# Gated linear recurrence of a two-block model: the diagonal step's products are issued ten weight chunks later, beside the third and fourth level

## The chip, the cores and the metric

The kernel runs on one core of one Trainium2 chip. The metric is the device time of one execution in microseconds (us). It is the median of three executions: 1901.26 us, from 1900.43 to 1902.49.

## The reference

The whole program is two transformer-like blocks over 256 tokens of width 2048: a convolution mixer, a recurrent mixer (HGRN2), windowed attention and a gated feed-forward layer. All matrix products are float32. The change is in the recurrent mixer alone, which is, for each of 16 heads of width 128, run once forwards and once backwards over the tokens:

```
def step(state, inp):
    qb, kb, vb, fb = inp
    b = jnp.cumsum(fb, axis=2)
    o_inter = jnp.einsum("bhtk,bhkv->bhtv", qb * jnp.exp(b), state)
    diff = b[:, :, :, None, :] - b[:, :, None, :, :]
    decay = jnp.exp(jnp.where(lower_tri, diff, -jnp.inf))
    scores = jnp.einsum("bhtk,bhsk,bhtsk->bhts", qb, kb, decay)
    o_intra = jnp.einsum("bhts,bhsv->bhtv", scores, vb)
```

The score of a pair of tokens is a product of query and key with a decay between them for every one of the 128 channels. Its diagonal (a token with itself) has no decay.

## The kernel before, in words

**The stream of weights.** Nearly the whole time goes into products of activations (256 tokens) with large weight matrices. A weight matrix is read in chunks of 256 rows by 512 columns; every chunk is one 512 KB transfer into one of four buffers `raw`. ScalarE rounds a chunk to `w_hi` (line 877), VectorE forms the rest `w_lo` (line 1261), and TensorE issues twelve matmuls for it (lines 619 to 621) into `acc`: two row tiles by two token tiles by three products (hi with hi, low with hi, hi with low). So TensorE may start a chunk when `split_ready` says that its `w_lo` is there, and ScalarE may round one when TensorE has left the chunk four before it.

**Hooks.** All else is hung between the chunks by hand. Each engine has its own table: `put(8, f)` runs `f` after the engine has issued its part of chunk 8 of a group of 32 chunks; numbers from 32 on fall in the next group. ScalarE and VectorE run some two to four chunks ahead of TensorE, so the same step has different numbers on different engines.

**The recurrence.** The 16 heads go in four groups `j` of four heads. The projections of group `j` are the 32 chunks of phase `hgrn` (use `j`); its recurrence is worked in the 32 chunks behind those (`process(j)`), thus beside the projections of group `j + 1`, and for the last group beside phase `hgrn_z`. VectorE first turns the raw projections (`quarters`, hooks 28, 30, 31, line 1549), GpSimd moves their blocks (`moves`, line 502), ScalarE makes gates and logarithms out of them (`gates`, `ln_f`, `ln_k`, lines 1046 to 1063), VectorE makes running sums (line 1442, 1449) and keys (1457, 1459). The pairs of tokens are then covered by eight levels and the diagonal. Level 1 is the pairs across the two halves of the sequence, level 2 those of neighbouring blocks of 64 tokens, level 3 of 32, down to level 8 of single tokens. For a level VectorE makes exponents (`diffs`), ScalarE takes their exponential (`exp`), VectorE weighs them with the queries (`weigh`, line 1499), TensorE forms the products (`level`, line 736; level 1 line 727), and the result is taken out of PSUM by ScalarE (`take`, lines 1089 to 1100, levels 0 to 3) or by VectorE under a mask (line 1508, levels 4 to 8). "Level 0" is the diagonal: its operand is made by `diagonal` on VectorE at hook 6, its products are 32 matmuls of 32x32 on TensorE at hook 8, and `take(j, 0)` on ScalarE at hook 11 copies them to `SB`, on which the masked copies of the levels from 4 on are laid. On TensorE level 1 stands at hook 13, level 2 at 14, levels 3 and 4 at 18, levels 5 and 6 at 22, levels 7 and 8 at 26 together with `av_across`, and `av` at 28.

Order between engines is held by semaphores that count: `g_G` operands weighed, `g_mm` levels multiplied, `g_S` levels taken, `g_M` moves of GpSimd. Operand buffers are `E` and `E_more` with two places each, chosen by `operands(s)`; before the change level 0 shares the second place of `E` with level 2. The PSUM tensor `T` has four banks: level 1 fills banks 0 and 1, the levels from 2 on alternate between banks 2 and 3, and level 0 uses bank 2.

Of the kernel before, what the change touches and what calls it, by code (L numbers as in the profile page):

```python
# [30 lines left out]
ACT = mybir.ActivationFunctionType  # L31
ALU = mybir.AluOpType
# [4 lines left out]
S = 256  # L37
# [127 lines left out]
def build(nc, t, out):  # L165
    ph = phases()
    ctx = ExitStack()
    with ctx:
# [75 lines left out]
        ssh = sb(hs, "ssh", [P, 3, 2 * HPG])  # L244
        powers = sb(hs, "powers", [P, 2 * HPG])
        gate_rows = (aftok, abtok, qtok, sz)
        lf_back = qtok[:, :, :].rearrange("p a (b c) -> p (a b) c", c=S)
        hs.close()

# [29 lines left out]

        def operands(s):  # L280

            b = (s - 1) % 4 if s else 1
            return (E_more if b >= 2 else E)[:, b % 2, :, :, :]

        def gate_banks(k):
            return T01 if k % 2 else T23
# [282 lines left out]
        def _(pe):  # L569
# [145 lines left out]
            def level(j, s):  # L715

                pe.wait_ge(g_G, 9 * j + s + 1)
                if s == 0:
                    pe.wait_ge(g_M, 3 * j + 3)
                if s >= 2:  # L720
                    pe.wait_ge(g_K, 7 * j + s - 1)
                    pe.wait_ge(g_S, 9 * j + s - 1)
                e = operands(s)
                for h in range(HPG):
                    for b in range(2):
                        if s == 1:
                            last = nc.tensor.matmul(T[:, h // 2, (h % 2) * S + b * P:(h % 2) * S + b * P + P],  # L727
                                                    e[:, 0, h, b * P:(b + 1) * P], e[:, 1, h, (1 - b) * P:(2 - b) * P],
                                                    start=True, stop=True)
                            continue  # L730
                        n = HB if s == 2 else QUARTER
                        for i in range(P // n):
                            at = b * P + i * n
                            to = b * P + (i ^ 1) * n if s in (2, 3) else at
                            g, q = (e[:, 1, h, at:at + n], qT[:, h, to:to + n]) if s == 0 else (e[:, 0, h, at:at + n], e[:, 1, h, to:to + n])
                            last = nc.tensor.matmul(T[i * n:(i + 1) * n, 2 + s % 2, (2 * h + b) * n:(2 * h + b + 1) * n],  # L736
                                                    g, q, start=True, stop=True)
                last.then_inc(g_mm, 1)

# [10 lines left out]

            def av_across(j):
                pe.wait_ge(g_raw, 4 * j + 4)
                pe.wait_ge(g_S, 9 * j + 2)
                av_products(True)

            def av(j):
# [2 lines left out]

            def process(j):  # L760

                at = Hooks().put(8, lambda: level(j, 0))
                for s in range(1, 9):
                    at.put(13 if s == 1 else 10 + 4 * (s // 2 + s % 2) if s > 2 else 14, lambda s=s: level(j, s))
                return at.put(26, lambda: av_across(j)).put(28, lambda: av(j))
# [98 lines left out]
        def _(act):  # L864
# [219 lines left out]

            def take(j, s):

                act.wait_ge(g_mm, 9 * j + s + 1)
                if s == 0:
                    A(SB[:, :, :, :].rearrange("p a b c -> p (a b c)"), T[:, 2, 0:S], ACT.Copy).then_inc(g_S, 1)
                    return  # L1090
                if s == 1:
                    if not is_first(j):
# [24 lines left out]
            def process(j):  # L1117
                at = Hooks().put(1, lambda: gates(j, 0)).put(6, lambda: gates(j, 1))
                for d in range(2):
                    at.put(6 + d, lambda d=d: ln_f(j, d)).put(8 + d, lambda d=d: ln_k(j, d))  # L1120
                at.put(11, lambda: take(j, 0)).put(12, lambda: cross_keys(j)).put(13, lambda: cross_queries(j))
                for s in range(1, 9):
                    if s > 1:
                        at.put(14 if s == 2 else 11 + 2 * s, lambda s=s: exp(j, s))
                    if s < ACT_TAKES:
                        at.put((15, 17, 20)[s - 1], lambda s=s: take(j, s))
                return at.put(29, lambda: blocks(j)).put(31, lambda: o_out(j))
# [112 lines left out]
        def _(dve):  # L1240
# [185 lines left out]
            def diagonal(j):  # L1426

                dve.wait_ge(g_lb, j + 1)
                dve.wait_ge(g_act, 6 * j + 2)
                for h in range(HPG):  # L1430
                    V.tensor_scalar(E[:, 1, 1, h, :], kf[:, h, :], lbj[:, 0, 1, h:h + 1], None, ALU.mult)
                settle()
                for h in range(HPG):
                    last = STT(out=E[:, 1, 1, h, :], in0=kb[:, h, :], scalar=lbj[:, 1, 1, h:h + 1],
                               in1=E[:, 1, 1, h, :], op0=ALU.mult, op1=ALU.add)
                last.then_inc(g_G, 1)

            def scan_f(j):
# [39 lines left out]
            def diffs(j, s):  # L1478

                e = operands(s)  # L1480
                dve.wait_ge(g_mm, 9 * j + max(1, s - 3))
                c = width(s)
                rf, rb = bounds(c)
                fr, bl = halves(Bc[:, :, :], c)[1], halves(Xc[:, :, :], c)[0]
# [16 lines left out]
            def take(j, s):  # L1501

                settle()
                if s == ACT_TAKES:
                    dve.wait_ge(g_S, 9 * j + s)
                dve.wait_ge(g_mm, 9 * j + s + 1)
                V.memset(none[:, :], 0.0)
                V.copy_predicated(SB[:, :, :, :].rearrange("p a b c -> p (a b) c"),
                                  lmask[:, s - ACT_TAKES, :].unsqueeze(1).to_broadcast([P, 8, QUARTER]),
# [301 lines left out]
```

## Time and profile before

| | |
|---|---|
| median of three executions | 1901.26 us |
| the profiled execution's own time | 1900.38 us |
| its span, first to last instruction | 1898.1 us |
| TensorE busy | 1892.3 us |
| VectorE, ScalarE, GpSimd busy | 1286.2, 1057.5, 613.3 us |

TensorE is recorded as busy over nearly the whole span. A matmul of the weight stream is recorded for 0.39 us, while the next one starts 0.23 us after it: records overlap, so a short wait of TensorE does not always show as idle time, and is better read from the distance of starts. Weight loads into the array (PEld) are recorded apart; idle time before one of them names what it waited for. A small float32 matmul of the levels is recorded twice, so a level of 32 shows as 64 records.

### The profile page before, as it was taken

The page shows a single profiled execution, that of the slowest core. Times are in us where ns is not written, and L with a number is a line of the kernel's source. Part 1 is how long each engine was busy: PE and PEld are TensorE (multiplying, and loading weights), DVE is VectorE, ACT ScalarE, POOL GpSimd, SP SyncE. Part 2 cuts the span into 40 slices and gives each one's busy share as a digit, 9 for nine tenths or more (in the row PEclk, how much of TensorE's full clock was granted, in tenths as well). Part 3 has the DMA queues.
Part 4 walks back from the last instruction along what each step waited for, and adds up shares of the span by engine and source line. Part 5 has one row for each costly group of instructions (what it writes and reads, how often), then busy time and mean ns, then how long its engine had stood idle before and what let it go on. Part 6 is the DMA issues. An engine that isn't in the chain of part 4 may idle for free.

```text
span 1898.1 us, 28814 instructions
## 1 busy us (share of the span) xinstructions
PE 1892.3 (100%) x10864; PEld 1560.7 (82%) x10864; DVE 1286.2 (68%) x1869; ACT 1057.5 (56%) x1401; POOL 613.3 (32%) x641
## 2 busy tenths in 40 slices
PE   9999999999999999999999999999999999999999
PEld 8888878888887888888887888888888888888887
DVE  5899967545888888887668876555555555544443
ACT  7444466455868787875465755444444444443432
POOL 1899852406051423302418641122222222210000
PEclk9999999999999999999999999999999999999999
DMA  9666556666555565555565455666666666666564
GB/s 324 192 190 188 178 167 195 193 189 188 167 166 170 155 186 162 175 160 185 189 190 151 151 177 169 208 190 197 189 190 197 192 195 190 195 192 196 191 195 159
DMA packets 183166, 352.62 MB, mean 186 GB/s; under 512 B 11792, under 2 KB 12304, under 8 KB 183056
## 3 DMA queue, kind: packets, MB, share of 16 engines
q1 hardware_dynamic: 182912, 351.12, 60.7%
q8 instruction: 72, 1.18, 0.3%
q14 instruction: 38, 0.31, 0.1%
q10 hardware_dynamic: 144, 0.01, 0.0%
HBM read 348.99 MB, written 2.10 MB: 185 GB/s over the span
## 4 chain that ended last, share of the span: by engine, by line
PE 91%; DVE 3%; POOL 2%; ACT 1%; issue 1%; DMA 1%; DVEq 1%; POOLq 0%; ACTq 0%; SPq 0%
PE acc L619 29%; PE acc L621 29%; PE acc L620 29%; PE T L736 1%; PE T L575 1%; DVE w_lo L1261 1%; POOL apad L524 1%; POOL kb L502 1%; DMA raw<-in_conv_w_in_dram 1%; DVEq L1247 1%; ACT w_hi L877 0%; POOL kf L502 0%; PE T L837 0%; PE T L727 0%; PE T L746 0%
## 5 line engine op out<-in xcount | busy, mean ns | idle before, releaser
L1261 DVE TENSOR_TENSOR w_lo<-raw,w_hi 128x1024 fp32r<-128x1024 f32 x564 | 695.3, 1235 | 518.6 <-ACT w_hi L877 510.7
L877 ACT ACTIVATE w_hi<-raw 128x1024 fp32r<-128x1024 f32 x656 | 688.9, 1058 | 610.8 <-PE acc L621 585.6
L619 PE MATMUL acc<-w_hi,h_hi 128*128 128x512 f32 x1872 | 736.0, 393 | 0.9 <-DVE w_lo L1261 0.8
L621 PE MATMUL acc<-w_hi,h_lo 128*128 128x512 f32 x1872 | 729.4, 390 | 0.0
L620 PE MATMUL acc<-w_lo,h_hi 128*128 128x512 f32 x1872 | 729.2, 390 | 0.0
L619 PEld LDWEIGHTS acc<-w_hi,h_hi 128*128 128x128 f32 x1872 | 351.6, 188 | 80.0 <-issue 5.8
L621 PEld LDWEIGHTS acc<-w_hi,h_lo 128*128 128x128 f32 x1872 | 351.5, 188 | 73.6
L620 PEld LDWEIGHTS acc<-w_lo,h_hi 128*128 128x128 f32 x1872 | 351.7, 188 | 71.1
L564 POOL COPY fT<-fq 32x256 f32<-32x256 f32 x176 | 110.8, 630 | 398.9 <-DVE fq L1743 392.0
L473 POOL TENSOR_TENSOR w_lo<-raw,w_hi 128x1024 fp32r<-128x1024 f32 x80 | 190.3, 2405 | 71.2 <-ACT w_hi L877 71.2
L1352 DVE SCALAR_TENSOR_TENSOR T<-vpad,feat,T 128x256 f32<-128x256 f32 x464 | 182.5, 485 | 0.0
L619 PE MATMUL acc<-w_hi,y_hi 128*128 128x512 f32 x384 | 151.1, 394 | 0.1
L620 PE MATMUL acc<-w_lo,y_hi 128*128 128x512 f32 x384 | 149.6, 390 | 0.0
L620 PE MATMUL acc<-w_lo,f_hi 128*128 128x512 f32 x352 | 137.0, 389 | 0.0
L619 PE MATMUL acc<-w_hi,f_hi 128*128 128x512 f32 x352 | 137.0, 389 | 0.0
L621 PE MATMUL acc<-w_hi,f_lo 128*128 128x512 f32 x352 | 137.0, 389 | 0.0
L502 POOL COPY kf<-sz 32x256 f32<-32x256 f32 x64 | 37.2, 582 | 279.1 <-DVEq L1247 276.6
L621 PE MATMUL acc<-w_hi,hy_lo 128*128 128x512 f32 x256 | 99.8, 390 | 0.0
L619 PEld LDWEIGHTS acc<-w_hi,y_hi 128*128 128x128 f32 x384 | 72.1, 188 | 17.0 <-issue 1.2
L620 PEld LDWEIGHTS acc<-w_lo,y_hi 128*128 128x128 f32 x384 | 72.2, 188 | 14.5
L621 PEld LDWEIGHTS acc<-w_hi,f_lo 128*128 128x128 f32 x352 | 66.1, 188 | 13.8
L619 PEld LDWEIGHTS acc<-w_hi,f_hi 128*128 128x128 f32 x352 | 66.1, 188 | 13.7
(252 smaller groups left out, 1553.8 us busy)
## 6 DMA issues: line engine op xcount, KB each, us to landing
raw<-in_hgrn_w_in_dram SPq DMA_DIRECT2D x160, 512.0 KB, 3.7
raw<-in_conv_w_in_dram SPq DMA_DIRECT2D x96, 512.0 KB, 4.2
raw<-in_ffn_w_gate_dram SPq DMA_DIRECT2D x88, 512.0 KB, 4.3
raw<-in_ffn_w_up_dram SPq DMA_DIRECT2D x88, 512.0 KB, 4.2
raw<-in_ffn_w_down_dram SPq DMA_DIRECT2D x88, 512.0 KB, 4.6
raw<-in_attn_w_qkv_dram SPq DMA_DIRECT2D x40, 512.0 KB, 3.8
raw<-in_conv_w_out_dram SPq DMA_DIRECT2D x32, 512.0 KB, 4.5
raw<-in_hgrn_w_out_dram SPq DMA_DIRECT2D x32, 512.0 KB, 3.9
```

Of the source, the lines that this page charges most:

```text
L473: nc.gpsimd.tensor_tensor(w_lo[:, slot, :, :], raw[:, slot, :, :], rounded(w_hi[:, slot, :, :]), ALU.subtract).then_inc(split_ready, 1)
L502: last = nc.gpsimd.tensor_copy(turned_block(dst, a, b), own_block(src, a, b))
L524: nc.gpsimd.tensor_copy(vrows[a * QUARTER:(a + 1) * QUARTER, b::4, :], kvtok[b * QUARTER:(b + 1) * QUARTER, :, KVH * HD:])
L564: last = nc.gpsimd.tensor_copy(turned_block(fT, a, b), own_block(fq, a, b))
L575: last = nc.tensor.transpose(dst[:, q // 2, at:at + P], src[:, tb, q * P:(q + 1) * P], ident[:, :])
L619: nc.tensor.matmul(o, hi[:, kt, a], w_hi[:, slot, kk, :], start=c == 0 and kk == 0, stop=False)
L620: nc.tensor.matmul(o, hi[:, kt, a], w_lo[:, slot, kk, :], start=False, stop=False)
L621: last = nc.tensor.matmul(o, lo[:, kt, a], w_hi[:, slot, kk, :], start=False, stop=c == p.chunks - 1 and kk == CK - 1)
L736: last = nc.tensor.matmul(T[i * n:(i + 1) * n, 2 + s % 2, (2 * h + b) * n:(2 * h + b + 1) * n], g, q, start=True, stop=True)
L877: A(w_hi[:, slot, :, :], raw[:, slot, :, :], ACT.Copy).then_inc(hi_ready, 1)
L1261: TT(w_lo[:, slot, :, :], raw[:, slot, :, :], rounded(w_hi[:, slot, :, :]), ALU.subtract).then_inc(split_ready, 1)
L1352: STT(out=cy[:, kt, :] if tap == TAPS - 1 else y, in0=v, scalar=w, in1=y, op0=ALU.mult, op1=ALU.add).then_inc(c_tap, 1)
```

## The change

The diagonal's products move on TensorE from hook 8 to hook 18, where they stand ahead of levels 3 and 4, and its copy on ScalarE from hook 11 to hook 20, ahead of the copy of level 3. The operand gets a buffer of its own (`same`, laid over the scratch tensor `fg`, not used otherwise in this stretch) and the products go to bank 0 of `T`, which is free once level 1 has been taken. Since `g_mm` and `g_S` count in order of issue, a function `place(s)` now gives the rank of a level: 1, 2, 0, 3, 4 and so on. VectorE's `diffs(j, 2)` no longer waits for level 0.

```
 def operands(s):
-    b = (s - 1) % 4 if s else 1
+    b = (s - 1) % 4
+def place(s):
+    return {1: 1, 2: 2, 0: 3}.get(s, s + 1)
...
 # TensorE, level(j, s)
                 if s == 0:
                     pe.wait_ge(g_M, 3 * j + 3)
+                    pe.wait_ge(g_S, 9 * j + place(1))
                 if s >= 2:
                     pe.wait_ge(g_K, 7 * j + s - 1)
-                    pe.wait_ge(g_S, 9 * j + s - 1)
+                    if s > 4:
+                        pe.wait_ge(g_S, 9 * j + place(s - 2))
+                    elif s > 2:
+                        pe.wait_ge(g_S, 9 * j + place(2))
+                    elif j:
+                        pe.wait_ge(g_S, 9 * j)
...
-                            g, q = (e[:, 1, h, at:at + n], qT[:, h, to:to + n]) if s == 0 else ...
-                            last = nc.tensor.matmul(T[i * n:(i + 1) * n, 2 + s % 2, ...
+                            g, q = (same[:, h, at:at + n], qT[:, h, to:to + n]) if s == 0 else ...
+                            last = nc.tensor.matmul(T[i * n:(i + 1) * n, 2 + s % 2 if s else 0, ...
...
 # TensorE, process(j)
-                at = Hooks().put(8, lambda: level(j, 0))
+                at = Hooks().put(18, lambda: level(j, 0))
...
 # ScalarE, take(j, s) and process(j)
-                act.wait_ge(g_mm, 9 * j + s + 1)
+                act.wait_ge(g_mm, 9 * j + place(s))
...
-                at.put(11, lambda: take(j, 0))
+                at.put(20, lambda: take(j, 0))
...
 # VectorE, diagonal(j): E[:, 1, 1, h, :] becomes same[:, h, :]; diffs(j, s):
-                dve.wait_ge(g_mm, 9 * j + max(1, s - 3))
+                if s > 4:
+                    dve.wait_ge(g_mm, 9 * j + place(s - 4))
```

On TensorE, before, at the first of the four groups: the diagonal's 32 matmuls (operands `qT` and `E`) stand alone behind chunk 8 of the weight stream.

```order
L620 MATMUL acc<-w_lo,h_hi 128x512
L621 MATMUL acc<-w_hi,h_lo 128x512
L736 MATMUL T<-qT,E 32x32 x32
L619 MATMUL acc<-w_hi,h_hi 128x512
L620 MATMUL acc<-w_lo,h_hi 128x512
```

On TensorE, after, behind chunk 18 of the same group: the diagonal's 32 matmuls (now with operand `fg`) are followed at once by the 32 of level 3 and the 32 of level 4, which the order shows as one row of 64 (`E_more`).

```order
L626 MATMUL acc<-w_hi,h_lo 128x512
L747 MATMUL T<-qT,fg 32x32 x32
L747 MATMUL T<-E_more 32x32 x64
L624 MATMUL acc<-w_hi,h_hi 128x512
L625 MATMUL acc<-w_lo,h_hi 128x512
```

So of two interruptions of the weight stream one is gone, and the other holds 96 small matmuls in place of 64.

On ScalarE, before, the copy into `SB` stands between the rounding of chunks 11 and 12, and the four pieces of level 3 (into `ST`) stand alone between the rounding of chunks 20 and 21.

```order
L877 ACTIVATE w_hi<-raw 128x1024
L1089 ACTIVATE SB<-T 128x256
L877 ACTIVATE w_hi<-raw 128x1024
...
L877 ACTIVATE w_hi<-raw 128x1024
L1100 ACTIVATE ST<-T 32x8x32 x4
L877 ACTIVATE w_hi<-raw 128x1024
```

On ScalarE, after, at the second place:

```order
L1094 ACTIVATE E_more<-E_more 128x1024 x2
L888 ACTIVATE w_hi<-raw 128x1024
L1100 ACTIVATE SB<-T 128x256
L1111 ACTIVATE ST<-T 32x8x32 x4
L888 ACTIVATE w_hi<-raw 128x1024
```

The copy now stands ahead of level 3's, and both ahead of the rounding of chunk 21. VectorE and GpSimd issue the same work in the same order as before.

## Rows read from the trace of the kernel before

**Rows 1.** The page: span, TensorE's busy time, the chain that ended last.

```profile
span 1898.1 us, 28814 instructions
...
PE 91%; DVE 3%; POOL 2%; ACT 1%; issue 1%; DMA 1%; DVEq 1%; POOLq 0%; ACTq 0%; SPq 0%
```

**Rows 2.** Timeline, TensorE, level 0 of the first group: start us, length us, instruction.

```profile
477.68 0.39 PE L620 MATMUL acc<-w_lo,h_hi 128*128 128x512 f32 x1
...
482.66 0.39 PE L621 MATMUL acc<-w_hi,h_lo 128*128 128x512 f32 x1
482.98 0.76 PE L736 MATMUL T<-qT,E 128*32 128x32 f32 x64
483.68 0.50 PE L619 MATMUL acc<-w_hi,h_hi 128*128 128x512 f32 x1
...
484.25 0.40 PE L621 MATMUL acc<-w_hi,h_lo 128*128 128x512 f32 x1
```

**Rows 3.** Timeline, TensorE, levels 3 and 4 of the first group.

```profile
513.91 0.39 PE L621 MATMUL acc<-w_hi,h_lo 128*128 128x512 f32 x1
514.23 1.37 PE L736 MATMUL T<-E_more 128*32 128x32 f32 x128
...
516.09 0.39 PE L621 MATMUL acc<-w_hi,h_lo 128*128 128x512 f32 x1
```

**Rows 4.** Waits before weight loads, 684 to 700 us: us in total, times, longest.

```profile
PEld acc L619 <- DVE w_lo L1261: 0.7, 2, 0.4
```

**Rows 5.** Timeline, TensorE, second group: start of chunks 10 and 13.

```profile
585.92 0.39 PE L621 MATMUL acc<-w_hi,h_lo 128*128 128x512 f32 x1
586.75 0.50 PE L619 MATMUL acc<-w_hi,h_hi 128*128 128x512 f32 x1 [0.44 <-DVE w_lo L1261]
...
594.84 0.39 PE L621 MATMUL acc<-w_hi,h_lo 128*128 128x512 f32 x1
595.28 0.50 PE L619 MATMUL acc<-w_hi,h_hi 128*128 128x512 f32 x1
```

**Rows 6.** Timeline, TensorE, first group: start of chunk 13.

```profile
494.71 0.39 PE L619 MATMUL acc<-w_hi,h_hi 128*128 128x512 f32 x1
```

**Rows 7.** Timeline, VectorE, first group: low part of chunk 13, then level 1's weighing.

```profile
492.71 1.22 DVE L1261 TENSOR_TENSOR w_lo<-raw,w_hi 128x1024 fp32r<-128x1024 f32 x1
494.89 1.23 DVE L1499 TENSOR_TENSOR E<-E,qT 128x1024 f32<-128x1024 f32 x1 [0.95 <-ACT E L1076]
```

**Rows 8.** Timeline, VectorE, second group: low parts of chunks 10 and 13.

```profile
585.47 1.23 DVE L1261 TENSOR_TENSOR w_lo<-raw,w_hi 128x1024 fp32r<-128x1024 f32 x1 [0.15 <-issue]
...
594.01 1.22 DVE L1261 TENSOR_TENSOR w_lo<-raw,w_hi 128x1024 fp32r<-128x1024 f32 x1
```

**Rows 9.** Timeline, ScalarE and VectorE, behind level 3 of the first group.

```profile
515.03 1.54 ACT L1100 ACTIVATE ST<-T 32x256 f32<-32x256 f32 x4 [1.90 <-PE T L736]
...
517.69 1.23 DVE L1261 TENSOR_TENSOR w_lo<-raw,w_hi 128x1024 fp32r<-128x1024 f32 x1 [0.79 <-ACT w_hi L877]
```

**Rows 10.** Stretches: us, then PE, PEld, DVE, ACT, POOL busy (count), PEclk, DMA share, GB/s.

```profile
517.60:541.60 24.00, 24.00 (x356) 19.92 (x355) 23.45 (x32) 17.30 (x19) 0.00 (x0) 1.00 0.56 157
541.60:569.00 27.40, 27.40 (x135) 23.08 (x133) 20.29 (x23) 17.18 (x21) 25.70 (x34) 1.00 0.55 164
569.00:595.30 26.30, 25.81 (x172) 20.09 (x170) 21.56 (x32) 24.74 (x44) 7.67 (x16) 1.00 0.54 169
```

**Rows 11.** Timeline, ahead of the second group's gates: VectorE's turning, GpSimd, ScalarE.

```profile
540.28 1.30 DVE L1549 STREAM_TRANSPOSE sz<-aftok 128x512 f32<-128x512 f32 x2
...
541.67 9.63 POOL L502 COPY kf<-sz 32x256 f32<-32x256 f32 x16 [67.49 <-DVEq L1247]
...
568.97 1.06 ACT L1046 ACTIVATE qtok<-kb 128x1024 f32<-128x1024 f32 x1 [1.64 <-POOL kb L502]
```

**Rows 12.** Timeline, ScalarE, first group: the diagonal's copy, and the next wait.

```profile
485.23 0.36 ACT L1089 ACTIVATE SB<-T 128x256 f32<-128x256 f32 x1
...
489.11 0.40 ACT L1070 ACTIVATE E<-kf,Bc 128x128 f32<-128x128 f32 x1 [1.27 <-DVEq L1247]
```

More of the change, by code:

```diff
@@ L246, in build @@
         gate_rows = (aftok, abtok, qtok, sz)
+        same = fg[:, :, :].rearrange("p a (b c) -> p (a b) c", c=S)
         lf_back = qtok[:, :, :].rearrange("p a (b c) -> p (a b) c", c=S)
@@ L734, in level @@
                             to = b * P + (i ^ 1) * n if s in (2, 3) else at
-                            g, q = (e[:, 1, h, at:at + n], qT[:, h, to:to + n]) if s == 0 else (e[:, 0, h, at:at + n], e[:, 1, h, to:to + n])
-                            last = nc.tensor.matmul(T[i * n:(i + 1) * n, 2 + s % 2, (2 * h + b) * n:(2 * h + b + 1) * n],
+                            g, q = (same[:, h, at:at + n], qT[:, h, to:to + n]) if s == 0 else (e[:, 0, h, at:at + n], e[:, 1, h, to:to + n])
+                            last = nc.tensor.matmul(T[i * n:(i + 1) * n, 2 + s % 2 if s else 0, (2 * h + b) * n:(2 * h + b + 1) * n],
                                                     g, q, start=True, stop=True)
@@ L752, in av_across @@
                 pe.wait_ge(g_raw, 4 * j + 4)
-                pe.wait_ge(g_S, 9 * j + 2)
+                pe.wait_ge(g_S, 9 * j + place(0))
                 av_products(True)
@@ L1085, in take @@
             def take(j, s):
-                act.wait_ge(g_mm, 9 * j + s + 1)
+                act.wait_ge(g_mm, 9 * j + place(s))
                 if s == 0:
-                    A(SB[:, :, :, :].rearrange("p a b c -> p (a b c)"), T[:, 2, 0:S], ACT.Copy).then_inc(g_S, 1)
+                    A(SB[:, :, :, :].rearrange("p a b c -> p (a b c)"), T[:, 0, 0:S], ACT.Copy).then_inc(g_S, 1)
                     return
@@ L1120, in process @@
                     at.put(6 + d, lambda d=d: ln_f(j, d)).put(8 + d, lambda d=d: ln_k(j, d))
-                at.put(11, lambda: take(j, 0)).put(12, lambda: cross_keys(j)).put(13, lambda: cross_queries(j))
+                at.put(20, lambda: take(j, 0)).put(12, lambda: cross_keys(j)).put(13, lambda: cross_queries(j))
                 for s in range(1, 9):
@@ L1430, in diagonal @@
                 for h in range(HPG):
-                    V.tensor_scalar(E[:, 1, 1, h, :], kf[:, h, :], lbj[:, 0, 1, h:h + 1], None, ALU.mult)
+                    V.tensor_scalar(same[:, h, :], kf[:, h, :], lbj[:, 0, 1, h:h + 1], None, ALU.mult)
                 settle()
                 for h in range(HPG):
-                    last = STT(out=E[:, 1, 1, h, :], in0=kb[:, h, :], scalar=lbj[:, 1, 1, h:h + 1],
-                               in1=E[:, 1, 1, h, :], op0=ALU.mult, op1=ALU.add)
+                    last = STT(out=same[:, h, :], in0=kb[:, h, :], scalar=lbj[:, 1, 1, h:h + 1],
+                               in1=same[:, h, :], op0=ALU.mult, op1=ALU.add)
                 last.then_inc(g_G, 1)
@@ L1504, in take @@
                 if s == ACT_TAKES:
-                    dve.wait_ge(g_S, 9 * j + s)
-                dve.wait_ge(g_mm, 9 * j + s + 1)
+                    dve.wait_ge(g_S, 9 * j + place(s - 1))
+                dve.wait_ge(g_mm, 9 * j + place(s))
                 V.memset(none[:, :], 0.0)
```

## The prediction

> **What bounds the kernel now.** I read the page first. The span is 1898.1 us and the chain that ended last is 91% TensorE [rows 1]: whatever is put into TensorE's row of work, or taken out, is time, unless TensorE waits somewhere near. So the second question is where TensorE waits around the moved step. Busy shares don't tell it, since records overlap; I went through the starts of its matmuls in the timeline.
>
> The undisturbed pace: 22 matmuls from 477.68 to 482.66 [rows 2], 0.226 us each, thus 2.72 us for a chunk of twelve.
>
> Where it waits: in the first of the four groups chunk 13 starts in step. In the second, chunk 10 starts 0.83 us behind the matmul before it and chunk 13 0.44 us [rows 5]; without the pace that is 0.60 and 0.21 us, plus 0.11 us each time because a first matmul behind a pause is recorded with 0.50 us where others have 0.39. The third group has two such waits for `w_lo`, 0.7 us together before the weight loads [rows 4], and the same view of 784 to 800 us gives the same row for the fourth. These are waits for VectorE, which finishes `w_lo` of chunk 13 at 594.01 + 1.22 = 595.23 us [rows 8]; TensorE starts 0.05 us later.
>
> What makes VectorE late there is what the forecast hangs on. I followed it backwards.
> - At 515.03 ScalarE takes level 3 of the first group, having waited 1.90 us for TensorE, and VectorE's next low part waits 0.79 us for ScalarE [rows 9].
> - From there VectorE is busy 23.45 of 24.00 us [rows 10], up to the turning at 540.28 [rows 11]; GpSimd, which had waited 67.49 us for that, starts at once and is busy 25.70 of 27.40 us [rows 10]; ScalarE waits 1.64 us for it until 568.97 [rows 11], and is itself busy 24.74 of 26.30 us up to chunk 13 of the second group [rows 10].
>
> So from level 3 of one group (TensorE's hook 18) to chunk 13 of the next, some 80 us, there is a second chain beside TensorE without room in it, and in groups two to four it is the longer one. From chunk 13 to hook 18 TensorE itself is the longer. The two form a circle.
>
> **The change part by part.**
>
> *Removed at hook 8.* From the last matmul before level 0 to the third behind it are 484.25 - 482.66 = 1.59 us [rows 2]; less three of the pace (0.68) the interruption costs 0.91 us. In group one TensorE then reaches chunk 13 0.91 us earlier than 494.71 [rows 6]. But `w_lo` of that chunk is done at 492.71 + 1.22 = 493.93 [rows 7], and with the 0.05 us above the start can be at 493.98 at the earliest. That gives 0.73 us, less 0.11 for starting behind a pause: 0.62 us gained. Does VectorE come earlier too? It doesn't wait for level 0 here, and ScalarE, which loses a copy of 0.36 us, next stands 1.27 us waiting for VectorE [rows 12]. So no. In groups two to four TensorE already waits for the same chunk, so 0.91 us less of work is 0.91 us more of waiting, mostly at chunk 10: gained 0.
>
> Level 1 behind chunk 13: it needs the weighing that ends at 494.89 + 1.23 = 496.12 [rows 7]; TensorE gets there at 493.98 + 0.11 + 12 x 0.226 = 496.80, so nothing new is late. The cover is 0.68 us thick.
>
> *Added at hook 18.* Levels 3 and 4 in one interruption cost 516.09 - 513.91 = 2.18 less 0.68, thus 1.50 us [rows 3]. One level alone costs 0.91, so a further one in the same interruption costs 0.59 us, and 0.32 us is the price of interrupting. The recorded lengths say the same: 0.76 us for 64 records, 1.37 us for 128 [rows 2, 3]. A third level of the same shape I take at 0.59, the nearest row; it would cost 0 if it hid wholly beside the others, for which no row speaks, and 0.91 us if it paid as one alone.
>
> Here the rule of the Trainium skill (TensorEngine Tiling (Array Packing), Key Properties) says that a change of tiling mode drains the TensorE. The trace agrees with it in kind: a level that joins others pays 0.32 us less than one alone. By that rule by itself, with TensorE as the only bound, the sum would be four times 0.32 us less; it is the first rival below.
>
> *Where the added 0.59 us goes.* Level 3 ends 0.59 us later relative to chunk 13, since level 0 now stands in front of it, and level 3's end is where the second chain begins. So all of that chain moves: chunk 13 of the next group comes 0.59 us later than it would.
>
> *The copy on ScalarE.* It now stands between the wait and level 3's copies, in the chain. It takes 0.36 us [rows 12] and can begin as soon as level 0 is done, 0.59 us before level 3 is; it is over 0.2 us before ScalarE is wanted. I cost it at nothing; uncovered it would be 0.36 us a group.
>
> *Waits.* Level 0's new wait is for the copy of level 1, five chunks back. Level 3 waits for the copy of level 2, as level 4 did directly behind it. On VectorE a wait that was never felt is gone. All nothing. Operand and bank are of the same kind and size as before.
>
> *Sum.* Group one: -0.62 + 0.59 = -0.03 us. Groups two, three and four: +0.59 us each, because nothing is gained at hook 8 and the circle or, behind the last, TensorE itself carries the addition to the end. Together +1.74 us. Against the profiled execution (1900.38 us, of which 1898.1 is span) that is 1902.1 us; the median of the runs is 0.88 us above that execution, so I put 1901.26 + 1.74 = 1903.0 us.
>
> **The rivals.**
>
> *The interruption is saved everywhere.* If the second chain has room that I don't see, TensorE alone counts: four times 0.32 us, thus -1.3 us, 1900.0 us. For it: group one does have 0.73 us of room. Against it: the waits of TensorE for `w_lo` in groups two to four. Chance 0.12.
>
> *Some of both.* The shift at hook 18 is swallowed in one or two groups by small gaps of the second chain (0.55 us of VectorE's 24.00 are not busy, mostly drains), so that the sum ends near 0: 1901.3 us. Chance 0.08.
>
> *The copy is not covered.* If ScalarE comes to level 3 late by the whole copy, 4 x 0.36 us more: +3.2 us, 1904.4 us. It decides where level 0's end and level 3's end lie less than 0.36 us apart. The pace of the small matmuls speaks against it. Chance 0.07.
>
> *Slower by more than the measurement's grain.* In group two TensorE would stand still at chunk 10 for 0.44 + 0.91 = 1.35 us instead of the 0.44 of [rows 5]. If its clock fell there from 2.4 to 1.2 GHz, each us of matmuls would take two. With +1.7 us already there, a further 2.1 us is needed for 0.2%, so 2.1 us of work at the low level; at 4 us of it the time is about 1905 us, and more if the shorter pauses of the third and fourth group do it too. Against it: the granted clock is 1.00 in the stretch with the pauses of today [rows 10]. Chance 0.03.
>
> *Forecast:* the second chain passes the addition on, +1.7 us. Chance 0.70, own range 1902.0 to 1904.2.
>
> **How the numbers follow.** A change of under 0.2% (3.8 us) can't be told from none by a measurement of this kernel. The forecast and the first three rivals lie inside it: 0.97, of which I give 0.03 to what I haven't thought of. Slower by over 0.2%: the clock, and the far end of the uncovered copy, 0.05. Faster: 0.01. No change: 0.94. The range runs from a little below the first rival, since medians of three move by about 1 us, to a little over the uncovered copy: 1899.6 to 1905.0.
>
> **What the changed profile would show.** TensorE waits at chunk 10 of groups two to four for 0.9 us longer than before, and in group one for the first time at chunk 13, some 0.2 us. The interruption at hook 18 costs 2.1 us net of the pace. ScalarE's `SB` copy ends before level 3's matmuls do. The distance from level 3 of one group to chunk 13 of the next is the same as before to 0.1 us, while that from chunk 13 to level 3 is 0.6 us longer. The forecast is wrong if chunk 13 of the second group comes earlier relative to level 3 of the first, if the three levels cost 0.91 us more than two, or if TensorE's clock is under 1.00 anywhere between 480 and 860 us.

## The result, and the profile after

The changed kernel takes 1908.68 us (median of 6 runs, 1906.29 to 1910.24) beside 1900.50 us of the kernel before (6 runs, 1899.72 to 1902.49): ratio 1.0037, 95% interval 1.0027 to 1.0047. That is slower by more than 0.2%, and outside the range of the prediction (up to 1905.0). The profiled execution took 1909.72 us.

The page of the changed kernel: the span, and the chain that ended last by engine.

```profile
span 1907.1 us, 28812 instructions
...
PE 83%; DVE 5%; POOL 4%; ACT 2%; issue 2%; DVEq 1%; POOLq 1%; DMA 1%; ACTq 0%; SPq 0%
```

The span is 9.0 us longer than that of [rows 1], and TensorE's share of the chain fell from 91 to 83%: more of the way to the end leads through VectorE and GpSimd.

To find the 9.0 us I compared the starts of the first matmul of the same chunk in both timelines:

```
start of                     after minus before, us     added since the row above
group one, chunk 0                 +0.28                (start-up)
group two, chunk 13                +0.34                +0.06
group two, chunk 19                +0.92                +0.58   hook 18
group two, chunk 27                +1.15                +0.23   hook 26
group three, chunk 10              +2.39                +1.24   second chain
group three, chunk 19              +3.03                +0.64   hook 18
group four, chunk 10               +4.12                +1.09   second chain
group four, chunk 19               +4.73                +0.61   hook 18
group four, chunk 23               +9.04                +4.31   behind hook 18
end of the span                    +8.97
```

Three rows at hook 18 are the predicted ones. Nearly half of the loss stands in one place behind hook 18 of the fourth group, and 2.3 us in the second chain, whose length the prediction had taken as fixed.

**The place in the fourth group.** Timeline of TensorE, changed kernel; the number in brackets is the idle time ahead of a row and what ended it.

```profile
820.98 0.39 PE L626 MATMUL acc<-w_hi,h_lo 128*128 128x512 f32 x1
821.21 0.40 PE L624 MATMUL acc<-w_hi,h_hi 128*128 128x512 f32 x1
824.01 0.50 PE L625 MATMUL acc<-w_lo,h_hi 128*128 128x512 f32 x1 [2.40 <-issue]
824.35 0.40 PE L626 MATMUL acc<-w_hi,h_lo 128*128 128x512 f32 x1
```

From 821.21 to 824.01 are 2.80 us, less one step of the pace 2.57 us. The releaser is "issue": no semaphore, buffer or bank that the profile shows was awaited. The next view says what did come in that time. DMA queues in the stretch 818 to 826 us, changed kernel: packets, MB, share.

```profile
q8 instruction: 1, 0.02, 0.7%
```

Queue 8 moves nothing but packets of 16,384 bytes. From the first of them to the one at 1264.6 us there are 64, and TensorE has 16,056 recorded instructions (matmuls, weight loads and its sequencer's) in that time: 255 for each packet. So I read a packet as a block of 256 instructions of TensorE's program code. This one started at 821.81 us and took 0.92 us by the DMA's record; TensorE went on 1.3 us after it. The block before had started at 808.63 us.

And behind the stop (the same kernel; stretches with the columns of [rows 10]):

```profile
818.00:821.00 3.00, 3.00 (x198) 2.52 (x197) 3.00 (x5) 1.44 (x4) 0.00 (x0) 1.00 0.77 227
821.00:824.00 3.00, 0.61 (x3) 0.17 (x1) 1.43 (x4) 2.96 (x5) 0.00 (x0) 1.00 0.28 107
824.00:825.00 1.00, 0.99 (x4) 0.85 (x5) 1.00 (x3) 1.00 (x2) 0.00 (x0) 0.95 0.27 33
825.00:827.00 2.00, 2.00 (x6) 1.53 (x6) 2.00 (x3) 0.37 (x1) 0.00 (x0) 0.50 0.82 254
827.00:828.00 1.00, 1.00 (x4) 0.82 (x3) 1.00 (x3) 0.82 (x1) 0.00 (x0) 0.50 0.45 55
...
829.00:832.00 3.00, 3.00 (x15) 2.49 (x14) 2.71 (x4) 2.24 (x3) 0.00 (x0) 1.00 0.47 115
```

After the stop the granted clock goes to 0.50, that is from 2.4 to 1.2 GHz: from 825.17 to 828.15 us the matmuls start 0.43 us apart instead of 0.23. With the slower steps at both ends of it that costs 1.6 us. Stop 2.57, clock 1.6, and 0.11 for starting behind a pause: 4.3 us, the whole row of the table.

**The pieces that the prediction named.** TensorE at hook 18 of the first group, then chunk 13 of the first and chunks 10 and 13 of the second group:

```profile
493.88 0.39 PE L626 MATMUL acc<-w_hi,h_lo 128*128 128x512 f32 x1
494.27 0.50 PE L624 MATMUL acc<-w_hi,h_hi 128*128 128x512 f32 x1
...
513.64 0.39 PE L626 MATMUL acc<-w_hi,h_lo 128*128 128x512 f32 x1
513.96 0.76 PE L747 MATMUL T<-qT,fg 128*32 128x32 f32 x64
514.57 1.35 PE L747 MATMUL T<-E_more 128*32 128x32 f32 x128
...
516.43 0.39 PE L626 MATMUL acc<-w_hi,h_lo 128*128 128x512 f32 x1
...
585.99 0.39 PE L626 MATMUL acc<-w_hi,h_lo 128*128 128x512 f32 x1
587.09 0.50 PE L624 MATMUL acc<-w_hi,h_hi 128*128 128x512 f32 x1 [0.72 <-DVE w_lo L1272]
...
595.16 0.39 PE L626 MATMUL acc<-w_hi,h_lo 128*128 128x512 f32 x1
595.62 0.50 PE L624 MATMUL acc<-w_hi,h_hi 128*128 128x512 f32 x1
```

ScalarE behind hook 18 of the first group, and what it takes there:

```profile
514.76 0.38 ACT L1100 ACTIVATE SB<-T 128x256 f32<-128x256 f32 x1 [1.90 <-PE T L747]
515.36 1.53 ACT L1111 ACTIVATE ST<-T 32x256 f32<-32x256 f32 x4 [0.22 <-PE T L747]
```

Three levels cost 516.43 - 513.64 = 2.79, less 0.68, thus 2.11 us, where two cost 1.50 in [rows 3]: 0.61 us for the third. The copy `SB` ends at 515.14, and ScalarE then waits another 0.22 us for level 3: it is covered. Chunk 13 of the first group starts 0.39 us behind the matmul ahead of it, a new short wait; VectorE's low part of that chunk ran from 492.99 to 494.21.

**The second chain.** The stretches of [rows 10] on its way from level 3 of group one to group two, moved along with it:

```profile
517.93:541.93 24.00, 24.00 (x356) 19.92 (x355) 23.45 (x32) 17.30 (x19) 0.00 (x0) 1.00 0.53 156
541.93:569.33 27.40, 27.40 (x135) 23.08 (x134) 20.29 (x23) 17.16 (x21) 25.71 (x34) 1.00 0.55 166
```

Between groups one and two it is the same chain, to 0.01 us of busy time. Between two and three it is not. GpSimd, and then VectorE, changed kernel:

```profile
667.80 3.27 POOL L507 COPY kb<-aftok 32x256 f32<-32x256 f32 x3
...
669.57 1.23 DVE L1272 TENSOR_TENSOR w_lo<-raw,w_hi 128x1024 fp32r<-128x1024 f32 x1 [0.74 <-ACT w_hi L888]
```

Three copies (the last three of the eight of this half of `kb`) take 3.27 us here; in e6, shown below, the same three take 2.18. The eighth copy started at 669.58 us, 0.01 us behind VectorE's low part of chunk 7, and took 1.49 us. A copy of this shape has two lengths, 0.4 to 0.5 us and 1.3 to 1.5 us: in the profiles of both kernels all 242 long ones started while a VectorE instruction with two inputs was running, and none of the 634 that started without one was long (84 started beside one and were short). In the kernel before, in the same transition, the copy came first and took 0.40, and the half of `kb` 9.10 instead of 10.20 us. Between groups three and four it is the same again, 9.98 for 9.01 us.

### The profile page after: what moved, and what is told of

Its sections match the earlier page's. It is cut to its first block, busy times and chain, and to the rows that moved or that the text cites. A ratio compares the mean times of both kernels' runs of the same rounds, so it can differ in the third digit from the quotient of the medians.

```text
span 1907.1 us, 28812 instructions
## 1 busy us (share of the span) xinstructions
PE 1895.4 (99%) x10864; PEld 1561.2 (82%) x10864; DVE 1286.6 (67%) x1869; ACT 1057.9 (55%) x1401; POOL 613.4 (32%) x641
## 4 chain that ended last, share of the span: by engine, by line
PE 83%; DVE 5%; POOL 4%; ACT 2%; issue 2%; DVEq 1%; POOLq 1%; DMA 1%; ACTq 0%; SPq 0%
PE acc L624 27%; PE acc L626 27%; PE acc L625 27%; POOL kb L507 2%; DVE w_lo L1272 2%; POOL kf L507 1%; DVEq L1258 1%; PE T L580 1%; POOL apad L529 1%; ACT w_hi L888 1%; PE T L747 1%; DMA raw<-in_conv_w_in_dram 1%; PE T L848 0%; PE T L738 0%; DVE Xc L1460 0%
```

## The experiments

Twelve runs. The kernel before is timed beside each set: 1900.64 us with e1 to e4, 1900.83 with e5 to e8, 1901.19 with e9 to e12. In the expectations, A is the theory that program code is late behind long bursts of small matmuls (its rival: a data wait that the changed order makes); D is that the second chain carries additions at hook 18 and TensorE's waits swallow those at hook 8; E that only TensorE's own work counts.

**Where the code stands: e1, e2, e3.** All kernels have the same work in the recurrence; only the position of its instructions in TensorE's code is moved, by tiny matmuls in front of the whole program, of which nothing is read. The shifts were worked out from the recorded instructions: four for a tiny matmul and four for a warming one.

```diff
-WARM = 14
+WARM = 10
+EXTRA = 36
...
+                for i in range(EXTRA):
+                    nc.tensor.matmul(T[0:QUARTER, 0, 0:QUARTER], ones[:, 0:QUARTER], ones[:, 0:QUARTER], start=True, stop=True)
```

e1 is the changed kernel moved by 128 instructions so; e2 the changed kernel with EXTRA = 64 and WARM = 8, moved by 232; e3 the kernel before moved as e1.

> The changed kernel with 36 tiny matmuls (32x32, of the constant ones) ahead of TensorE's warming up and 10 warming matmuls instead of 14: all later TensorE instructions lie 128 further on in its program, and the work is the same. Theory A (the 2.6 us stop of TensorE at 821.2 us, after the three levels of the fourth group, is a wait for program code, which comes in blocks of 256 instructions; a burst of 384 recorded instructions in 2.1 us outruns it where the code already fetched ends 300 to 415 instructions behind the burst's first): now this holds for groups one (400), two (355) and three (310) and no longer for four. Two to three stops of 2 to 5 us, so 4 to 12 us slower than the changed kernel: 1912 to 1920 us. Theory B (the stop has to do with that place's data or semaphores): one stop at the same place of the fourth group, 1908 us as before.

> The same with 64 tiny matmuls and 8 warming ones: later instructions 232 further on. Theory A: fetched code ends at about 507, 462 and 417 behind the first small matmul in groups two to four and at 552 or 296 in group one: no stop, or one under 1 us; with it goes the low clock behind the stop (1.6 us in the profile). So about 4 us faster than the changed kernel: 1903 to 1905 us. Theory B: the stop stays, 1908 us.

> The kernel before with the same shift of 128 instructions. Control. Theory A: its largest burst is 256 recorded instructions, which the fetched code covers wherever it ends, so no stop: within 1 us of the kernel before. If merely shifting code moves the time of any kernel by some us (theory C: every shift has a price or the start-up is worse), it is seen here too.

Measured: e1 1910.86 us (1909.94 to 1912.76), ratio 1.0053, 1.0039 to 1.0067. Timeline of TensorE at hook 18 of groups two, three and four:

```profile
618.21 0.76 PE L750 MATMUL T<-qT,fg 128*32 128x32 f32 x64
618.82 1.22 PE L750 MATMUL T<-E_more 128*32 128x32 f32 x113
623.31 0.33 PE L750 MATMUL T<-E_more 128*32 128x32 f32 x15 [3.27 <-issue]
...
722.90 0.76 PE L750 MATMUL T<-qT,fg 128*32 128x32 f32 x64
723.51 1.03 PE L750 MATMUL T<-E_more 128*32 128x32 f32 x90
727.18 0.54 PE L750 MATMUL T<-E_more 128*32 128x32 f32 x38 [2.65 <-issue]
...
825.03 0.76 PE L750 MATMUL T<-qT,fg 128*32 128x32 f32 x64
825.64 1.35 PE L750 MATMUL T<-E_more 128*32 128x32 f32 x128
```

The stops now stand in groups two and three, in the middle of a run of products that wait for nothing between them, and group four has none; in group one there is one behind the burst (1.87 us). Between one product of level 4 and the next there is no data wait to blame, and the gap moved by 23 records from one group to the next. That speaks against the rival. More than that, the stops stand where the expectation put the end of the fetched code. It named 400, 355 and 310 instructions behind the burst's first; in the trace TensorE has 399, 355 and 310 recorded instructions (products and their weight loads) from there to the stop. The median, 1910.86 us, is a little under the 1912 to 1920 expected.

e2: 1907.51 us (1906.17 to 1908.57), 1.0035, 1.0023 to 1.0047. The stop left group four, but one of 1.73 us stands in group one, where none or less than 1 us was expected:

```profile
515.70 0.95 PE L750 MATMUL T<-E_more 128*32 128x32 f32 x83
518.38 0.60 PE L750 MATMUL T<-E_more 128*32 128x32 f32 x45 [1.73 <-issue]
```

So the median gained only 1.2 us, where some 4 were expected; the first group also starts 1.15 us later than in the changed kernel. The expectation had left the end of the code in group one open, at 552 or 296 instructions; the stop came behind 295. The size was missed because the second of the two held.

e3: 1902.44 us (1900.56 to 1904.91), 1.0009, 1.0000 to 1.0018. No stop; the 1 us is there at the start of the first group already. Bursts of two levels did not stop at either position, and the padding itself costs 1 us, which belongs to e1 as well. The median is 1.8 us above the kernel before, where under 1 was expected: its profile is 0.98 us late at the first group, 1.04 behind the fourth and 1.95 at its end, and the last 0.9 us are not explained.

**The burst itself: e4 and e11.** e4 is the changed kernel with the diagonal step half a chunk earlier, so that six large matmuls stand between it and level 3; e11 is the kernel before with level 3's products issued twice, so that its burst is as long as the changed kernel's, without any other part of the change.

```diff
-                at = Hooks().put(18, lambda: level(j, 0))
+                at = Hooks().put(17.5, lambda: level(j, 0))
```
```diff
-                for h in range(HPG):
+                for h in tuple(range(HPG)) * (2 if s == 3 else 1):
```

> The changed kernel with level 0 on TensorE half a chunk earlier (hook 17.5), thus again an interruption of its own; ScalarE's copy stays at hook 20. No burst of three levels, same position of all code. Theory A: no stop and no low clock, but 0.91 us instead of 0.59 in the circle for each of three groups: 4.2 us less and 1.0 us more than the changed kernel, about 1905 us. If the lateness comes from the second chain (the added time behind chunk 13, plus turns of 1 us in GpSimd's moves of kb), 1905 to 1906; if it were from the burst alone, it would fall back to 1901.

> The kernel before with level 3's products issued twice at hook 18: a burst of 384 recorded instructions, and level 0 still alone at hook 8. Theory A, with the place at which fetched code ends taken from the changed kernel's profile: it ends 399, 482, 309 and 392 instructions behind the burst's first in groups one to four, so stops of 2 to 4 us in groups one, three and four and none in group two. With 0.6 us of work a group and part of the lost time taken back where TensorE waits anyway: 1906 to 1914 us. Without A: 4 x 0.6 us, 1903 us, and no stop.

e4: 1905.42 us (1903.10 to 1906.15), 1.0021, 1.0012 to 1.0030, no row with the releaser "issue" (one matmul in group four starts 0.13 us late), granted clock 1.000 over the run: 3.3 us faster than the changed kernel, though each separate interruption costs 0.9 us instead of 0.6. That was the expectation. It is still above the prediction's range: the stop alone doesn't explain the miss.

e11: 1909.87 us (1908.36 to 1912.00), 1.0047, 1.0033 to 1.0061. TensorE at hook 18 of groups two to four:

```profile
614.48 1.90 PE L736 MATMUL T<-E_more 128*32 128x32 f32 x192
...
714.82 1.56 PE L736 MATMUL T<-E_more 128*32 128x32 f32 x154
719.12 0.54 PE L736 MATMUL T<-E_more 128*32 128x32 f32 x38 [2.75 <-issue]
...
819.15 1.90 PE L736 MATMUL T<-E_more 128*32 128x32 f32 x192
824.57 0.50 PE L620 MATMUL acc<-w_lo,h_hi 128*128 128x512 f32 x1 [2.39 <-issue]
```

Groups one (0.47 us), three and four stop, group two does not, as expected. The expectation put the ends of the code at 399, 309 and 392; the stops stand behind 398, 309 and 392 recorded instructions. With level 0, its buffer, its bank and its waits all as before, the length of the burst alone makes the stops.

Over all profiles there are eleven waits of TensorE of 0.2 us or more with the releaser "issue" at hook 18: one in the changed kernel, three in e1, one in e2, three in e11, and one each in e7, e9 and e10 below. Every one ends 1.2 to 1.5 us behind the end of a packet on queue 8, whether it lasted 0.20 or 3.27 us. That is what a wait for this packet looks like.

**What is added at hook 8: e5.** The kernel before with level 0's products issued twice at hook 8:

```diff
-                for h in range(HPG):
+                for h in tuple(range(HPG)) * (2 if s == 0 else 1):
```

> The kernel before with level 0's 32 products issued twice at hook 8 (same operands, same result), 128 more recorded instructions for each of four groups. Theory D (the second chain: behind hook 8 TensorE waits for VectorE in groups two to four anyway, so work there is free): +0.6 us in group one, which has no wait, 0 to +0.2 in the others: about +0.7 us against the kernel before. Theory E (TensorE alone sets the time, its small work costs where it stands): 4 x 0.59 = +2.4 us.

1902.08 us (1900.87 to 1902.57), 1.0005, 0.9996 to 1.0014. The median is 1.25 us above the kernel before, between the two forecasts, and its interval holds both no change and 2.4 us; the profile says more. There group one loses 0.53 us, group two 0.07, group three at most 0.1. The level's record is 0.54 us longer (1.30 us below, 0.76 in [rows 2]), and in groups two and three the waits of TensorE swallow it. Group four comes 1.0 us later, but there GpSimd's eighth copy collides (1.47 us), which it does not in that transition of the kernel before, so this group tests nothing. That work taken out at hook 8 gains nothing in group two is shown by the changed kernel's own rows above.

```profile
482.98 1.30 PE L736 MATMUL T<-qT,E 128*32 128x32 f32 x128
```

**The second chain made shorter: e6, e9, e10.** ScalarE takes level 3 (in e9 and e10 the diagonal's copy too) one chunk later, behind the rounding of that chunk's weights, so that a rounding no longer waits behind a wait for TensorE. e6 is the kernel before so, e9 the changed kernel, e10 is e4 so.

```diff
-                        at.put((15, 17, 20)[s - 1], lambda s=s: take(j, s))
+                        at.put((15, 17, 21)[s - 1], lambda s=s: take(j, s))
```

> The kernel before with ScalarE's copy of level 3 one chunk later (hook 21), so that the rounding of chunk 21 no longer stands behind a wait of 1.9 us for TensorE. Theory D: VectorE's low part of chunk 21 comes 0.79 us earlier, with it the whole second chain, and TensorE's waits at chunks 10 and 13 of groups two to four (1.0, 0.4, 0.4 us) shrink: -1.2 to -1.8 us, 1899 us. Theory E: no change, since TensorE does the same work in the same order.

> The changed kernel with ScalarE's copies of level 0 and level 3 one chunk later (hook 21). Theory D (second chain): VectorE's low part of chunk 21 no longer waits for TensorE's burst, so the 0.6 us added at hook 18 doesn't go into the chain and the chain is 0.8 to 1.4 us shorter in each of three groups: about 3 to 4 us faster than the changed kernel, with the stop for code in the fourth group still there: 1904.5 to 1906. Without D: 1908 to 1909.

> Both remedies: level 0 half a chunk earlier on TensorE (no burst of three levels, hence no stop for code) and ScalarE's copies at hook 21. Theories A and D together: what is left is TensorE's own work, where the kernel before has an interruption at hook 8 and this one has it at 17.5; TensorE's waits at chunks 10 and 13 are a little longer than in the kernel before with the same copy at hook 21. 1898.5 to 1900.5 us, 3 to 7 us under the changed kernel's level and above the 1898.2 of the kernel before with the later copy. Without A or D: 1904 and more.

e6: **1898.21 us** (1897.70 to 1898.65), 0.9985, 0.9976 to 0.9994, faster than both kernels. Its page, its ScalarE and its GpSimd:

```profile
PE 96%; DVE 1%; ACT 1%; POOL 1%; DMA 1%; DVEq 0%; issue 0%; POOLq 0%; ACTq 0%; SPq 0%
```
```profile
512.21 1.99 ACT L877 ACTIVATE w_hi<-raw 128x1024 fp32r<-128x1024 f32 x2
...
515.15 1.54 ACT L1100 ACTIVATE ST<-T 32x256 f32<-32x256 f32 x4 [0.95 <-PE T L736]
...
664.67 2.18 POOL L502 COPY kb<-aftok 32x256 f32<-32x256 f32 x3
```

The rounding `w_hi` now stands ahead of the wait for level 3, and VectorE has its next low part at 516.94 instead of 517.69 [rows 9]. The chain that ended last is 96% TensorE, and the view of waits names none for TensorE's matmuls between 480 and 880 us, where in the changed kernel six for `w_lo` stand (3.2 us). Its runs lie within 0.95 us; those of the kernel before within 2.7. The median is 2.6 us lower, more than expected (1.2 to 1.8). The later copy has a second effect that was not expected: GpSimd's eighth copy now starts 0.12 to 0.36 us ahead of VectorE and takes 0.40 us in all three transitions, where one collides in the kernel before. What each of the two effects gives was not separated.

e9: 1903.68 us (1901.62 to 1905.71), 1.0014, 1.0005 to 1.0023, 5.0 us faster than the changed kernel and a little better than the 1904.5 to 1906 expected. The stop in group four stays (2.29 us); the granted clock stays at 1.00 behind it, and no transition collides, which the expectation had not counted. e10: 1901.31 us (1900.94 to 1902.10), 1.0001, 0.9992 to 1.0011; 4.1 us faster than e4, but 0.8 us short of what was expected. It still has a small wait for code in group four (0.20 us), and no collision. With both remedies together the kernel with the moved step gets back to the time of before, and no further. (Gains against the changed kernel or e4 are across sets, between which the kernel before itself moves by up to 0.7 us.)

**The near tie on GpSimd: e7 and e8.** e7 is the changed kernel with a small write by VectorE ahead of the low part of chunk 7, so that GpSimd's copy comes first; e8 the kernel before with two drains on GpSimd ahead of its moves, so that it comes second.

```diff
+                    if name == "hgrn" and i == 7:
+                        V.memset(spare[:, 0:LATE], 0.0)
```
```diff
+                nc.gpsimd.drain()
+                nc.gpsimd.drain()
```

> The changed kernel with a memset of 128 columns on VectorE (about 0.15 us, of a spare tensor) before the low part of chunk 7 of each hgrn group. Theory F (GpSimd's eighth block copy of the second half of kb takes 0.4 us when it starts before VectorE's low part of chunk 7 and 1.4 us when it starts behind it, and in the changed kernel it started 0.01 to 0.11 us behind in all three groups): now it starts first in all three, its half of kb takes 9.1 us instead of 10.1, ScalarE's gates come 1.0 us earlier and TensorE's waits at chunk 10 shrink by as much. The stop for code in the fourth group stays. About 3 us faster than the changed kernel: 1905.7 us. Without F: no change or 0.4 us slower.

> The kernel before with two more drains on GpSimd between the first and second half of kb's moves, so that these start some 0.1 us later. Theory F: the eighth copy now starts behind VectorE in all three groups (before: in one of three), kb's second half takes 10.1 us three times, and TensorE's waits in groups three and four grow by 1.0 us: +2 us, about 1902.7. Without F: +0.1 us a group at most.

e7: 1907.31 us (1906.91 to 1907.88), 1.0034, 1.0021 to 1.0046. In two of the three transitions the copy now came first, took 0.40 us and the half of `kb` 9.0 instead of about 10.1 us; chunk 10 of group two starts 1.1 us earlier against the kernel before than in the changed kernel. The third still collided, the stop of group four stayed, and the median is 1.4 us lower where 3 were expected. e8: 1900.60 us (1898.80 to 1902.16), 0.9998, 0.9989 to 1.0007. Its profiled execution, the slowest of its runs, collides in all three transitions, and chunk 10 of the next group comes 1.1 us later each time in two of them; but the median did not move. Inconclusive on what the tie costs over many executions. The price in one execution is clear: of the 42 transitions in all fourteen profiles, the eighth copy started 0.01 to 0.11 us behind VectorE in 18 and took 1.38 to 1.49 us each time; in the other 24 it started ahead and took 0.40.

**The buffer alone: e12.** The kernel before, level 0 where it was, its operand in a buffer over `fg`:

```diff
-                    last = STT(out=E[:, 1, 1, h, :], in0=kb[:, h, :], scalar=lbj[:, 1, 1, h:h + 1],
+                    last = STT(out=same[:, h, :], in0=kb[:, h, :], scalar=lbj[:, 1, 1, h:h + 1],
```

> The kernel before with the diagonal's operand in its own buffer and nothing moved (hook 8, second bank of the pair, copy at hook 11). If the time comes from the place in the order alone, as theories A and D say: within 1 us of the kernel before. If the buffer laid over the scratch tensor costs something (reads or writes that collide), it shows here.

1901.01 us (1899.37 to 1902.24), 0.9998, 0.9989 to 1.0008: no cost that these runs can tell.

## Why the prediction was wrong, point by point

**Right: hook 8 in group one.** Forecast: start of chunk 13 0.05 us behind `w_lo`, a pause price of 0.11, -0.62 us in all; with the move at hook 18, -0.03. Measured: 494.27, with `w_lo` done at 494.21. Against a start-up that was 0.28 us later, chunk 13 came 0.44 us earlier, so 0.72 us were gained at hook 8, 0.1 more than forecast, and group one as a whole cost about 0.05 us.

**Right: hook 8 in groups two to four.** The extra time of TensorE there became waiting. It was split: chunk 10 of group two waits 0.72 us by the row, 0.28 more than in [rows 5], and the rest stands as a shorter pause of 0.39 us at chunk 9, so the 1.35 us in one piece that I named did not occur. The weight loads of the third group wait for `w_lo` 2.4 us where [rows 4] have 0.7, in part because of the collision told below, from which the rows of groups three and four can't be parted:

```profile
PEld acc L624 <- DVE w_lo L1272: 2.4, 3, 1.1
```

**Right: hook 18 passes on 0.59 us.** Measured +0.58, +0.64 and +0.61 us in groups two to four, the third level itself 0.61. The copy on ScalarE and the waits cost nothing, as put (the rows above), and so does the buffer (e12).

**The step that failed: "A third level of the same shape I take at 0.59, the nearest row; it would cost 0 if it hid wholly beside the others, for which no row speaks, and 0.91 us if it paid as one alone."** The bounds held for TensorE's work, but left out its supply. Two levels are 256 recorded instructions (products and weight loads) in 1.4 us, three are 384 in 2.1 us. Code comes in blocks of 256 (255 recorded instructions a packet, above), and in all four groups of the changed kernel the next block was started only 3.3 to 3.45 us behind the burst's start and was there 1 us later. Whether TensorE runs dry before depends on where the fetched code ends. From the stop of group four (behind 393 recorded instructions) and the positions of the instructions I estimate that end at 528, 483, 438 and 393 instructions behind the start of the burst in groups one to four: only the fourth stops. (By position alone group one could also be 272; but no packet of queue 8 starts between 2.2 us ahead of that burst and 3.4 us behind its start, when TensorE has 399 instructions behind it, and it doesn't stop.) In e1 the ends moved and the stops with them; in e11 I estimated 399, 309 and 392 for the groups that stop and 482 for the one that does not. All seven stops of e1, e2 and e11 stand within one recorded instruction of an end worked out before the run. In the changed kernel this is 2.6 us, and the half clock behind it 1.6 us more. e1 (it moves), e4 (it goes when the burst is split) and e11 (it comes without the change) show it.

The Trainium skill (Runtime: NRT & Kernel Launch, Instruction fetch mechanics) says that each engine's instruction memory is refilled in 16 KiB blocks of 256 instructions over a queue of its own, and that the fetch is hidden because instructions are dispatched more slowly than they are filled. The trace agrees with the block (16,384 bytes and 255 recorded instructions a packet), and with the queue (queue 8). It disagrees with "hidden": behind or in bursts of 384 instructions in 2.1 us there are waits of 2.40 us (the changed kernel) and 2.75 us (e11) with the releaser "issue". The measurement decides.

**The fourth rival** had named the clock, and had it at the wrong place. The pauses at chunks 9 and 10 (0.39 and 0.72 us) left the granted clock at 1.00; it fell behind the stop of 2.57 us. The price, 1.6 us, was of the size that I had given (2.1 us of work lost for slower by 0.2%), but I had no mechanism that stops TensorE that long, hence 0.03. My sum there also mixed two measures: 4 us of time at the low level cost 2 us and give 1905 us, 4 us of work at it would give 1907. The last sign that I named, a clock under 1.00 between 480 and 860 us, is the one that came, at 825 us.

**A second assumption failed: that the second chain's length is fixed** ("The distance from level 3 of one group to chunk 13 of the next is the same as before to 0.1 us"). That held from group one to two (both kernels collide there) and failed twice behind, by 1.2 and 1.1 us; the 0.23 us at hook 26 of the second group I can't attribute. In each of the two one copy of GpSimd starts 0.01 and 0.11 us behind a VectorE instruction and takes 1.49 and 1.38 us instead of 0.40. e7, which puts the copy first, gave 1.1 us back at chunk 10 of the second group.

The Trainium skill (SBUF — State Buffer, SBUF: two separate sides) describes such a thing: GpSimd and a VectorE instruction with two SBUF inputs share a port pair, and whichever starts first holds it for its whole instruction. The trace agrees: `w_lo<-raw,w_hi` has two inputs and takes 1.23 us, and in all fourteen profiles every eighth copy that starts behind it is 1.0 to 1.1 us longer, and every one that starts ahead of it takes 0.40. In that order it is VectorE's record that is longer: 1.46 us where the copy was 0.01 us ahead (the kernel before, third transition).

**The account:** start-up 0.28, group one 0.05, three times hook 18 1.83, group two's 0.23, two collisions 2.33, stop and clock 4.31: 9.0 us. Forecast were 1.74 of it. Without the stop and the collisions the profiled execution would have taken 1903.1 us.

**What stays open.** That the change causes the two further collisions, and so 2.3 us of the loss, is not shown. One profile is one execution: the changed kernel collides in three of three transitions and e4 too, the kernel before in one, but e12, which has its order and its time, in two. e8, meant to force it, left the median alone. Nor do I know what starts the fetch of a block; only that in the changed kernel it came 3.3 to 3.45 us behind the burst's start, and in one group each of e1 and e2 and in two of e11 already 1.0 to 1.6 us behind it. And the six runs of the changed kernel differ by 3.9 us: the two with a mean clock of 1.000 (1906.29 and 1907.58) are the two shortest, so the fall of the clock probably does not follow every stop. The other profiles show that it doesn't: it followed waits of 1.87 and 3.27 us in e1, 2.39 and 2.75 us in e11 and 2.75 us in e7, and not those of 2.65 us (e1, group three), 2.29 us (e9) and 1.73 us (e2). The length of the wait alone does not decide it; what does is open.

## What to carry to other kernels

A burst of small matmuls has a second price beside TensorE's time: its instructions. When steps are gathered in one place, count the instructions per us and look in the profile for waits with the releaser "issue" and for the code queue's packets beside them; half a chunk of large matmuls between two bursts (e4) cost 0.3 us and took away a stop of 2.6. Any change of the code ahead of such a place can move the stop, so a gain or loss of a few us should be tried at a second code position before it is put down to the change.

Work that stands where TensorE waits anyway is nearly free (0.07 to 0.1 us of 0.54 in e5's second and third groups), and moving it behind the start of the chain for which it waits costs its full time. The better edit was the opposite one: take from the second chain, by letting no rounding stand behind a wait for TensorE in ScalarE's order (e6, -2.6 us).

## What the runs showed of the hardware

- A burst of 384 TensorE instructions in 2.1 us can outrun its code: waits of 0.47 to 3.27 us in the changed kernel, e1, e2 and e11, none in bursts of 256 in 1.4 us at two code positions (the kernel before and e3). TensorE went on 1.2 to 1.5 us behind the end of the packet, each time.
- After a stop of 2.57 us the granted clock was 0.50 for 3 us; after waits of 0.72 us it stayed at 1.00, and after one of 2.65 us (e1) and one of 2.29 us (e9) too.
- A 32x256 copy on GpSimd takes 0.40 us, and 1.38 to 1.49 us if VectorE's `w_lo<-raw,w_hi`, with two inputs, started 0.01 to 0.11 us before it (18 of 18 cases). 0.01 us decided over 1 us of the span.
